# Keys and values ahead of queries, as one 512-wide product, in the second attention of a two-block transformer kernel

## The reference, cut to what matters

```python
# end of layer 0
gate = jax.nn.sigmoid(rms_norm_2(h, ln_ple[0]) @ ple_w_gate[0])
h = h + (gate * (p[0] @ ple_w_proj[0])).astype(h.dtype)
# layer 1
xn = rms_norm_2(h, ln_mix[1])
k, v = jnp.split(rms_norm_2(h, kv_norm) @ w_kv, 2, axis=-1)     # 1024 x 512
k = rms_norm_2(to_heads(k, 4), k_gain)                          # 4 key heads of 64
q = rms_norm_2(to_heads(xn @ w_q, 16), q_gain) * 64 ** -0.5     # 16 query heads of 64
# one block of 256 keys: causal attention with a slope per head
s = q @ k.T - slope * distance
o = softmax(s) @ v
h = h + o @ w_out
h = h + hier_moe(rms_norm_2(h, ln_ffn[1]), ...)                 # 32 experts, two chosen per token
```

## Time and profile before

| | us |
|---|---|
| median of 3 runs | 1100.78 (1098.12 to 1101.6) |
| profiled execution, its own time | 1101.6 |
| profiled execution, its span | 1099.8 |
| TensorE busy | 1041.1 (95%) |
| VectorE busy | 752.0 (68%) |
| ScalarE busy | 714.6 (65%) |
| GpSimd busy | 104.7 (10%) |

### The profile page before, as it was taken

The page is one execution under the profiler, slowest core; times in us unless marked ns, Lnnn a source line. Parts: engine busy times, 40 slices in busy tenths (PEclk is TensorE's granted clock), DMA queues, the critical chain, the costliest instruction groups (busy, mean ns, idle before and its releaser), DMA issues.

```text
span 1099.8 us, 17528 instructions
## 1 busy us (share of the span) xinstructions
PE 1041.1 (95%) x6168; PEld 873.2 (79%) x6168; DVE 752.0 (68%) x1315; ACT 714.6 (65%) x1232; POOL 104.7 (10%) x189
## 2 busy tenths in 40 slices
PE   7988899999998997899999999999989899999998
PEld 6877789999997885797787778867878687887766
DVE  4686567666666564556668888877756668878876
ACT  5665644444446443576679899957667669888955
POOL 9018000000000020000140000000010140000000
PEclk9999999999999997999999999999999999999999
DMA  9871047555637444003519999955322518999950
GB/s 296 275 249 39 1 135 229 186 181 187 185 120 245 145 154 153 1 1 108 219 43 331 334 336 347 328 178 163 119 83 99 227 39 318 334 342 331 331 182 39
DMA packets 106157, 209.25 MB, mean 190 GB/s; under 512 B 7737, under 2 KB 51745, under 8 KB 105825
## 3 DMA queue, kind: packets, MB, share of 16 engines
q1 hardware_dynamic: 103584, 204.04, 53.9%
q0 software_dynamic: 2064, 3.25, 1.1%
q10 hardware_dynamic: 432, 0.99, 0.2%
HBM read 207.19 MB, written 1.06 MB: 189 GB/s over the span
## 4 chain that ended last, share of the span: by engine, by line
PE 82%; DVE 6%; ACT 5%; issue 3%; DMA 2%; POOL 1%; SPq 0%; ACTq 0%; DVEq 0%; POOLq 0%
PE bank L869 22%; PE bank L1572 16%; PE bank L1591 10%; PE bank L1245 8%; PE bank L1255 8%; PE bank L967 4%; PE bank L948 2%; PE bank L956 2%; DMA expert_w<-in_moe_w_up 2%; PE bank L775 1%; PE bank L2093 1%; PE bank L947 1%; PE bank L1613 1%; PE bank L1080 1%; PE bank L1402 1%
## 5 line engine op out<-in xcount | busy, mean ns | idle before, releaser
L869 PE MATMUL bank<-weight_parts,x_high 128*128 128x512 f32 (+2 forms) x768 | 223.9, 376 | 9.4 <-DVE weight_parts L890 2.8
L1572 PE MATMUL bank<-expert_high,block_high 128*128 128x256 f32 x560 | 183.5, 328 | 3.4 <-ACT block_low L1520 2.4
L1500 DVE TENSOR_TENSOR expert_low<-expert_w,expert_high 128x1024 fp32r<-128x1024 f32 x140 | 164.6, 1218 | 10.2 <-ACT expert_high L1493 10.0
L869 PEld LDWEIGHTS bank<-weight_parts,x_high 128*128 128x128 f32 x768 | 140.1, 189 | 36.5 <-ACT x_high L839 6.9
L1572 PE MATMUL bank<-expert_high,block_low 128*128 128x256 f32 x560 | 158.1, 282 | 0.0
L1572 PE MATMUL bank<-expert_low,block_high 128*128 128x256 f32 x560 | 158.0, 282 | 0.0
L890 DVE TENSOR_TENSOR weight_parts<-ring,weight_parts 128x1024 fp32r<-128x1024 f32 (+3 forms) x112 | 121.4, 1104 | 47.7 <-ACT weight_parts L887 47.1
L887 ACT CAST weight_parts<-ring 128x1024 fp32r<-128x1024 f32 (+3 forms) x112 | 104.1, 956 | 74.3 <-PE bank L869 65.3
L1493 ACT CAST expert_high<-expert_w 128x1024 fp32r<-128x1024 f32 x140 | 140.0, 1053 | 17.4 <-DMA expert_w<-in_moe_w_up 17.0
L869 PE MATMUL bank<-weight_parts,x_low 128*128 128x512 f32 (+2 forms) x384 | 143.9, 375 | 0.0
L1591 PE MATMUL bank<-expert_w,junk 128*128 128x512 f32 x280 | 131.3, 593 | 0.0
(11 more groups left out here) (353 smaller groups left out, 1757.0 us busy)
## 6 DMA issues: line engine op xcount, KB each, us to landing
expert_w<-in_moe_w_gate SPq DMA_DIRECT2D x70, 512.0 KB, 5.6
expert_w<-in_moe_w_up SPq DMA_DIRECT2D x70, 512.0 KB, 7.3
expert_w<-in_moe_w_down SPq DMA_DIRECT2D x70, 512.0 KB, 5.4
ring<-in_w_ff SPq DMA_DIRECT2D x64, 512.0 KB, 3.8
ring<-in_w_in SPq DMA_DIRECT2D x16, 512.0 KB, 8.3
ring<-in_a_w_in SPq DMA_DIRECT2D x16, 512.0 KB, 4.5
ring<-in_ple_w_gate SPq DMA_DIRECT2D x16, 512.0 KB, 5.7
ring<-in_w_o SPq DMA_DIRECT2D x8, 512.0 KB, 3.9
```

Source lines behind the costliest of these rows:

```text
L869: mm = nc.tensor.matmul(bank[:, j["m"] % 4, 0:n], j["operand"][x][:, 2 * c + kk, at[0]:at[1]], weight_parts[:, number % PAIRS, w, kk * n:( ...
L1500: nc.vector.tensor_tensor(half_of(expert_low[:, b % DEPTH, 0:2048], j), half_of(expert_w[:, b % DEPTH, 0:2048], j), half_of(expert_high[:, ...
L1572: mm = nc.tensor.matmul(bank[:, 4 + b % 2, 0:256].rearrange("p (q n) -> p q n", q=2), x[:, b % 2, k, :], w[:, k], start=k == 0 and n == 0, ...
```

## The change

Keys and values become one product of 512 columns (`l_kv`) with its own transposes ahead of it, and it comes before the queries. The order on TensorE is: `t_kv`, `l_kv`, `t_moba`, all of `l_q`, then the transposes of the keys and of the query heads; the wait for all evictions now stands ahead of these. The first splits move with it: ScalarE issues two, behind all four gate evictions, where it issued three between them; VectorE issues one ahead of the last four gate instructions, where it issued three. The keys' squares, root and scaling move forward, the keys' turn is taken before the last query heads are squared, and the preload of the Exp table goes. The ring gets 12 loads for these products instead of 16.

```diff
--- before.py
+++ after.py
@@ -615,20 +615,18 @@
 
     moe_and_ple(0)
     n_moba = norm([(h, rows, D_MODEL)])
+    t_kv = turn(h, KB, [(kv_high, gains["kv_norm"], kv_low)])
     t_moba = turn(h, KB, [(x_high, gains["ln_mix1"], x_low)])
+    l_kv = linear(a["w_kv_shared_2"], KB, 512, (kv_high, kv_low), moba_kv, "copy", n_moba)
     l_q = linear(a["b_w_q_2"][0], KB, D_MODEL, x_parts, moba_q, "copy", n_moba)
-    t_kv = turn(h, KB, [(kv_high, gains["kv_norm"], kv_low)])
-    l_k = linear(a["w_kv_shared_2"], KB, 256, (kv_high, kv_low), moba_kv, "copy", n_moba, at=0)
-    l_v = linear(a["w_kv_shared_2"], KB, 256, (kv_high, kv_low), moba_kv, "copy", n_moba, at=256)
-    run(l_q + l_k + l_v)
-    r_mq = [root(16, DIM), root(16, DIM)]
-    r_mk = root(8, DIM)
+    run(l_kv + l_q)
+    r_mk, r_mq = root(8, DIM), [root(16, DIM), root(16, DIM)]
     mq = heads(moba_q, 16, 64)
     mk = heads(moba_kv[:, :, 0:256], 4, 64)
     mqT, mkT = turned_heads(0, 8, P), turned_keys(8)
+    t_mk = turn_keys(heads(moba_kv[:, :, 0:256], 2, P), mkT, head_gain[:, 7:8])
     t_mq = [turn_heads(heads(moba_q[:, :, 512 * g:512 * g + 512], 4, P), 4, mqT[:, 4 * g:4 * g + 4], head_gain[:, 6:7])
             for g in range(2)]
-    t_mk = turn_keys(heads(moba_kv[:, :, 0:256], 2, P), mkT, head_gain[:, 7:8])
     t_mix3 = turn(mix, KB, [(x_high, None, x_low)])
     l_moba_o = linear(a["b_w_out_2"][0], KB, D_MODEL, x_parts, h, "add")
     moe_and_ple(1)
@@ -1846,10 +1844,9 @@
         split_first(act, l_gate[layer], "act", 2)
         wait_units_added(act, layer + 1)
         act_norm(act, n_ple[layer])
-        take_linear(act, l_gate[layer][:2], "act")
+        take_linear(act, l_gate[layer], "act")
         if layer == 0:
-            split_first(act, l_q, "act", 0, 3)
-        take_linear(act, l_gate[layer][2:], "act")
+            split_first(act, l_kv, "act", 0, 2)
         act.wait_ge(ple_done, 4 * (layer + 1))
 
     def dve_moe_and_ple(dve, layer):
@@ -1872,7 +1869,7 @@
         for g in range(2):
             take_linear(dve, l_gate[layer][2 * g:2 * g + 2], "dve")
             if layer == 0 and g == 1:
-                split_first(dve, l_q, "dve", 0, 3)
+                split_first(dve, l_kv, "dve", 0, 1)
             cols = slice(g * 512, (g + 1) * 512)
             for t in range(TILES):
                 wait_took(dve, l_gate[layer][2 * g + t:2 * g + t + 1])
@@ -2015,11 +2012,10 @@
         scale_heads(g, nkw, scales(r_nk, 4, 4), pool_scaled)
         pool_clear_acc(pool, 0)
         pool_steps(pool, 0)
-        pool.wait_ge(scale_ready, 8)
+        pool.wait_ge(scale_ready, 6)
         scale_heads(g, mk, scales(r_mk, 0, 4), pool_scaled)
         pool.wait_ge(pool_scaled, 5)
-        pair_of_keys = max(n for n in l_v[0]["splits"] if n % PAIRS == 1)
-        pool.wait_ge(lin_made, splits[pair_of_keys]["made"])
+        pool.wait_ge(lin_made, l_q[-1]["made"])
         clear_keys(mkT)
         pool_clear_acc(pool, 1)
         pool_steps(pool, 1)
@@ -2129,19 +2125,17 @@
         pe_turn(pe, t_mix2)
         pe_linear(pe, l_nsa_o, t_mix2)
         pe_moe_and_ple(pe, 0)
-        pe_turn_tiles(pe, t_moba, [(ple_done, 3), (ple_done, 4)])
-        pe_linear(pe, l_q[0:2], t_moba)
-        pe_turn(pe, t_kv)
-        pe_linear(pe, l_q[2:4])
-        pe_linear(pe, l_k, t_kv)
-        pe_linear(pe, l_v)
+        pe_turn_tiles(pe, t_kv, [(ple_done, 3), (ple_done, 4)])
+        pe_linear(pe, l_kv, t_kv)
+        pe_turn(pe, t_moba)
+        pe_linear(pe, l_q, t_moba)
+        wait_took(pe, l_kv + l_q)
+        pe.wait_ge(pool_scaled, 5)
+        pe_turn(pe, t_mk)
         for g in range(2):
             pe.wait_ge(dve_scaled, 4 + g)
             pe_turn(pe, t_mq[g])
-        pe.wait_ge(pool_scaled, 5)
-        pe_turn(pe, t_mk)
         wait_turned(pe, t_mk + t_mq[0] + t_mq[1])
-        wait_took(pe, l_v)
         pe.wait_ge(keys_cleared, 8)
         pe_attention(pe, att_m)
         pe.wait_ge(mixed, n_heads[0] // 4)
@@ -2272,30 +2266,30 @@
         nc.scalar.preload_act_table(ACT.Sqrt)
         wait_took(act, l_nsa_o)
         act_moe_and_ple(act, 0)
+        take_turn(act, t_kv, "act")
+        split_first(act, l_kv, "act", 2)
+        act_norm(act, n_moba)
+
+        take_linear(act, l_kv, "act")
         take_turn(act, t_moba, "act")
-        split_first(act, l_q, "act", 3)
-        act_norm(act, n_moba)
-
+        wait_took(act, l_kv)
+        for t in range(TILES):
+            squares(work[:, t * 256:(t + 1) * 256], moba_kv[:, t, 0:256], last=t == 1)
+        take_linear(act, l_q[0:2], "act")
+        act.wait_ge(sums_ready, 7)
+        act_root(act, r_mk)
         for g in range(2):
-            take_linear(act, l_q[2 * g:2 * g + 2], "act")
+            if g:
+                take_turn(act, t_mk, "act")
             wait_took(act, l_q[2 * g:2 * g + 2])
             for t in range(TILES):
                 squares(rows[:, g, t * 512:(t + 1) * 512], moba_q[:, t, g * 512:(g + 1) * 512], last=t == 1)
+            act.wait_ge(sums_ready, 8 + g)
+            act_root(act, r_mq[g])
             if g == 0:
-                take_turn(act, t_kv, "act")
-            act.wait_ge(sums_ready, 7 + g)
-            act_root(act, r_mq[g])
-        take_linear(act, l_k, "act")
-        wait_took(act, l_k)
-        for t in range(TILES):
-            squares(work[:, t * 256:(t + 1) * 256], moba_kv[:, t, 0:256], last=t == 1)
-        act.wait_ge(sums_ready, 9)
-        act_root(act, r_mk)
-        take_linear(act, l_v, "act")
-        nc.scalar.preload_act_table(ACT.Exp)
+                take_linear(act, l_q[2:4], "act")
         take_turn(act, t_mq[0], "act")
         take_turn(act, t_mq[1], "act")
-        take_turn(act, t_mk, "act")
         act_attention(act, att_m)
         split_first(act, l_moba_o, "act", 0, 1)
         take_turn(act, t_mix3[:2], "act")
@@ -2487,29 +2481,34 @@
         take_linear(dve, l_nsa_o[2:], "dve")
         wait_took(dve, l_nsa_o)
         dve_moe_and_ple(dve, 0)
+        take_turn(dve, t_kv[:1], "dve")
+        split_first(dve, l_kv, "dve", 1, 2)
+        take_turn(dve, t_kv[1:3], "dve")
+        split_first(dve, l_kv, "dve", 2, 3)
+        take_turn(dve, t_kv[3:], "dve")
+        split_first(dve, l_kv, "dve", 3)
+        dve_norm(dve, n_moba)
+        take_linear(dve, l_kv, "dve")
         take_turn(dve, t_moba, "dve")
-        split_first(dve, l_q, "dve", 3)
-        dve_norm(dve, n_moba)
+        dve.wait_ge(squared, 7)
+        v.tensor_reduce(r_mk["sum"], work[:, 0:512].rearrange("p (h d) -> p h d", d=64), AX.X,
+                        ALU.add).then_inc(sums_ready, 1)
+        take_linear(dve, l_q[0:2], "dve")
+        dve_root(dve, r_mk, scale_ready)
         for g in range(2):
-            take_linear(dve, l_q[2 * g:2 * g + 2], "dve")
-            dve.wait_ge(squared, 7 + g)
+            if g:
+                take_turn(dve, t_mk, "dve")
+            dve.wait_ge(squared, 8 + g)
             v.tensor_reduce(r_mq[g]["sum"], rows[:, g, :].rearrange("p (h d) -> p h d", d=64), AX.X,
                             ALU.add).then_inc(sums_ready, 1)
-            if g == 0:
-                take_turn(dve, t_kv, "dve")
             dve_root(dve, r_mq[g], scale_ready)
-            dve.wait_ge(scale_ready, 6 + g)
+            dve.wait_ge(scale_ready, 7 + g)
             steepen(r_mq[g], 8 * g, 8)
             scale_heads(v, mq[:, :, 8 * g:8 * g + 8, :], scales(r_mq[g], 0, 8), dve_scaled)
-        take_linear(dve, l_k, "dve")
-        dve.wait_ge(squared, 9)
-        v.tensor_reduce(r_mk["sum"], work[:, 0:512].rearrange("p (h d) -> p h d", d=64), AX.X,
-                        ALU.add).then_inc(sums_ready, 1)
-        dve_root(dve, r_mk, scale_ready)
-        take_linear(dve, l_v, "dve")
+            if g == 0:
+                take_linear(dve, l_q[2:4], "dve")
         take_turn(dve, t_mq[0], "dve")
         take_turn(dve, t_mq[1], "dve")
-        take_turn(dve, t_mk, "dve")
         dve_attention(dve, att_m)
         split_first(dve, l_moba_o, "dve", 0, 1)
         take_turn(dve, t_mix3[:2], "dve")
```

## The result

| | before | after |
|---|---|---|
| median, run beside each other (us) | 1101.19 (4 runs) | 1119.20 (1114.68 to 1121.94, 4 runs) |
| ratio, 95% interval | | 1.0155 [1.0120, 1.0190] |
| profiled execution / its span | 1101.60 / 1099.8 | 1117.53 / 1115.5 |
| mean granted clock | 0.986 | 0.977 |

Over both sets the change costs 1.1 to 1.9%.

A forecast was written before the change was run, and what follows sets the result against it. TensorE, 82% of the chain that ended last, was taken to bound the kernel. Terms -4.97 + 3.23 + 2.46 + 6.4 + 1.0 gave +8.1, with the clock +11.7: 1112.5 us beside the median, range 1105 to 1118.

The forecast's parts named there:

- One product: Keys and values in 48 wide matmuls, 11.01 us, instead of 96 narrow ones and a gap, 15.98: saves 4.97 us.
- The split ahead of the gated add: At the gate, VectorE's low half waits for ScalarE's later cast and delays the multiply: costs 3.23 us, bounds 2.5 to 4.
- The second operand: Ahead of the query product, TensorE waits for VectorE's takes of the second transposes: costs 2.46 us, bounds 1.7 to 3.
- The tail: From last product to first score, the queries' uncovered chain takes 10.4 us against 4.0: costs 6.4, bounds 5 to 8.
- The ring: Ahead of routing, expert weights load later because slots shift by four, delaying the last residual add: 1.0 us, bounds 0 to 2.5.
- The Exp table: Ahead of the first Exp, the table load without preload is covered with 0.4 us to spare: costs nothing.
- The clock: Behind three new waits, low clock for 3.3 us at three chances in four: costs 3.6 us, bounds 0 and 7.
- the clock did not hold: Rival: TensorE keeps full clock through the new waits, so the sum is +8.1, 1108.9 us; chance 0.2.
- The late loads: Rival: the second expert's weights land 3 us later, ahead of the residual adds: +14.7, 1115.5 us; chance 0.11.
- No wait was hidden: Denies the rival that ScalarE and VectorE run ahead and hide the three product hand-overs: 1096.8 us; chance 0.06.

The follow-up runs named there:

- both sets: The changed kernel's first four runs (1.0155, median 1119.20 us) and the same kernel unaltered, run again (1.0135, median 1115.93 us), each against the kernel before.
- e10: Changed kernel with 26 matmuls of zeros in its last wait alone, ahead of the last head transposes; 1.0113 to the kernel before.
- e9: Changed kernel with 16 matmuls of zeros in its first wait alone, at the gate; 1.0127 to the kernel before.
- e6: Kernel before with the keys' evictions and values' first splits moved ahead of the second query half's root; 0.9973 to the kernel before.
- e5: Kernel before with one 512-wide key/value product in the old place behind the queries, output projection's loads at slot 0; 1.0009 to the kernel before.
- e2: Changed kernel with matmuls of zeros (16, 9 and 26, results unused) in all three waits; 1.0097 to the kernel before.
- e4: Changed kernel with ScalarE squaring the last queries ahead of its take of the keys; 1.0133 to the kernel before.
- e3: Changed kernel with the output projection's loads starting again at slot 0 of the ring; 1.0122 to the kernel before.
- e11: Changed kernel run again unaltered, on the same chip as two of the fill runs; 1.0135 to the kernel before, median 1115.93 us.
- e1: Changed kernel with ScalarE casting the first two pairs of key weights between the gate evictions again; 1.0094 to the kernel before.
- e8: Kernel of e6 with matmuls of zeros (9, 13 and 5) in three waits of the compressed branch; 0.9950 to the kernel before, 1094.85 us.

## Why the prediction was right and wrong

Direction, mechanism and places were right, and the size of one term was not: 1112.5 was forecast, up to 1118, and the first set came to 1119.2, the second to 1115.9. That one set lies outside the range and the other inside it is in part the luck of the runs.

- *One product*: -4.97 forecast. At full clock the new product takes 10.97 and 10.98 (e10, e9) for the 11.01 assumed. Right. Little of it is the form, by e6 0.50 us (11.51 for 96 narrow, 11.01 for 48 wide) and not the 0.8 that I read from the first 48 narrow ones; e5 and e6 show that the rest is the gap and the clock behind it.
- *The split ahead of the gated add*: 3.23 forecast, 3.23 measured. Here the trace of before carried the whole answer: who stands behind whom on ScalarE and VectorE.
- *The second operand*: 2.46 forecast, 2.44 measured.
- *The tail*: 6.4 forecast. Without the clock it is 10.60 (e2) less 4.01, 6.6. Up to the scaling's end the chain ran as laid out, 8.56 us behind the last product against 8.7. The 0.2 come after it: the last take of query heads waits 0.40 for the transposes made behind the scaling (e2), where I had the two takes in a row. e4 shows that the order of squares and keys' take is 1.0 of the tail.
- *The ring*: 1.0 forecast, 1.52 measured, and e3 gives it back whole. The casts waited for the DMA twice (3.52, 1.83).
- *The Exp table*: nothing, as the row said. The Trainium skill (ScalarE: Activation LUTs, "What ACT_TABLE_LOAD costs") would have had a drain of 1.38 us besides; the load here stands 0.02 behind the instruction before it, so the trace shows no drain.
- *The clock*: 3.6 forecast, 6.5 in the profile up to the end of attention (0.58 + 2.24 + 1.64 + 0.9 + 1.10), and 6.4 by e2. This is the step that failed: "at three chances in four: 3 x 0.75 x 1.6". All three waits brought the lower level, not three in four, and two of the falls lasted three times the 3.3 us that I priced, at a cost of 2.8 and 2.0 instead of 1.6. The earlier trace rows had one of that kind, 13.1 us from 428.5. What comes right behind the first and third wait is broken work (transposes, 0.77 of idle, single steps of attention), as there; that alone doesn't set the length, since the first fall was short in e3 and e10 with the same work behind it. What does set it stays open. The upper bound of 7 was right, and the range should have had it at its full value. Its high end was also added up loosely: 8.1, 6 of clock in all and 1.5 more for the loads give 1116.4 beside the median, not 1118.

Without the clock my sum was +8.1. The table has -5.0 + 3.23 + 2.44 + 6.6 + 1.52 = 8.8 in its place, 0.7 more, mostly the ring. Against the profiled 1117.5 I was 4.2 short (1113.3), of which the clock is 2.9. The Trainium skill (TensorE: Matmul & The Clock Gate, "What's actually happening") says that the number of matmuls that run slow at a kernel's start differs from run to run, with the moment at which they meet a monitor that runs freely. The trace agrees for a wait inside a kernel: 3.4 and 10 us at the same place in runs of the same instructions. The times of the changed kernel lie between 1112.5 and 1121.9, those of the kernel before, over all sets, between 1097.7 and 1103.1. The medians of its two sets are 3.3 us apart, half of what 1112.5 is off the first; that this is the clock's doing fits the runs (1112.54 at a mean granted clock of 0.984, 1119.96 at 0.974) and is not shown run by run.

The rivals: the clock did not hold (with it held in the stage, e2 has 1.0097, where that rival's 1108.9 is 1.0074). The late loads cost 0.5 us more than forecast, not 3. No wait was hidden: all three show as idle time, in full.

## What to carry to other kernels

A new wait on the bounding engine costs its own length and can bring a low clock with it. Here each of the three waits did, for 0.6 to 2.8 us; only the range can be given, since the same wait gave either end in different runs. Before an order is turned round, look at which product covers which chain, and keep a product that nothing waits for as cover at the end; moving one eviction (e6) gave more here than the whole new order. And where slots or buffers are handed out in a ring, count what each later prefetch lands on.

## What the runs showed of the hardware

- With one and the same wait of 4.30 us the lower clock lasted 3.4 us in two profiles (e3, e10) and 10.2 in three (the changed kernel, e4, e11); with one of 6.23 it was 10.2 in five (the changed kernel, e1, e3, e9, e11).
- The length of a wait doesn't say whether the clock falls. The wait of 2.20 us ahead of the query product brought a fall in all seven profiles that did not fill it; the one of 2.2 us from 95.7, ahead of the first attention, brought one in a single profile of thirteen (e1, low from 98.9 to 102.3), with the same instructions in all.
- Matmuls of zeros in the waits kept the granted clock at 1.00 and gave back 6.4 us in a stage of 62 (e2). In the compressed branch they gave 2.5 (e8): 64 matmuls of 128 columns took 7.38 us at full clock, 0.115 each, against 9.98.
- A table load did not wait for what its activation waited for: it ran at 823.09, 3.3 us ahead of the Exp that needs it.
